# Group-2 projections of tiles 4 to 7 gathered ahead of tile 6, one attention step at a time in the mixer opening, norms of tiles 4 to 7 at one in four steps

## The reference, cut to what matters

```python
h = rms_norm(x, norm_mix_g)
a_b, a_c, a_v, q, k, v, g_a, g_b = split(h @ w_in)        # 512,512,512, 768,768,768, 1024,1024
y_a = (a_b * causal_dwconv(a_c * a_v)) @ w_proj_a
# attention: 12 heads of 64 in 3 groups; group g looks back over (window, dilation) =
# (128, 1), (512, 4), (2048, 16); the three groups of a head slot are mixed by their softmax denominators
y_b = mixed(attention(q, k, v)) @ w_proj_b
x = x + (sigmoid(g_a + b0) * y_a + sigmoid(g_b + b1) * y_b) @ w_out
h = rms_norm(x, norm_ffn_g)
gate, val = split(causal_dwconv(h @ w_up))
out = rms_norm(x + (silu(gate) * val) @ w_down, final_norm_g)
```

## Time and profile before

| | |
|---|---|
| time before, median of 3 runs | 1995.62 us |
| lowest | 1995.58 us |
| the profiled execution | 1993.38 us |
| its span on the slowest core (core 2) | 1991.5 us |
| spans of the eight cores | 1979.9 to 1991.5 us |
| PE busy in the span | 1939.1 us, 97% |
| DVE, ACT, POOL busy | 57%, 42%, 32% |

### The profile page before, as it was taken

The page is one execution under the profiler, slowest core; times in us unless marked ns, Lnnn a source line. Parts: engine busy times, 40 slices in busy tenths (PEclk is TensorE's granted clock), DMA queues, the critical chain, the costliest instruction groups (busy, mean ns, idle before and its releaser), DMA issues.

```text
span 1991.5 us, 38036 instructions; the slowest of 8 cores (1979.9 to 1991.5 us)
## 1 busy us (share of the span) xinstructions
PE 1939.1 (97%) x11662; PEld 1021.4 (51%) x11662; DVE 1140.3 (57%) x1754; ACT 835.4 (42%) x1679; POOL 645.8 (32%) x1431
## 2 busy tenths in 40 slices
PE   5899989999999999999999999999999999999998
PEld 4566656655555444444445555655444444444443
DVE  2456653565445534435236676858684939577582
ACT  2455663452122222121224554636462627355361
POOL 1544430001111021120234354545452626344341
PEclk9899999999999999999999999999999999999999
DMA  9658988385538624525468933131422222221201
GB/s 174 175 152 204 236 203 143 98 185 126 145 100 178 162 59 124 133 48 136 75 186 184 169 104 80 49 102 54 122 60 84 75 85 70 59 96 33 85 1 53
DMA packets 196045, 229.49 MB, mean 115 GB/s; under 512 B 116916, under 2 KB 139322, under 8 KB 195464
## 3 DMA queue, kind: packets, MB, share of 16 engines
q1 hardware_dynamic: 178056, 192.86, 35.7%
q0 software_dynamic: 17792, 34.20, 11.5%
HBM read 161.90 MB, written 72.57 MB: 118 GB/s over the span
## 4 chain that ended last, share of the span: by engine, by line
PE 88%; DMA 4%; issue 2%; POOL 1%; DVE 1%; ACT 1%; SPq 1%; POOLq 0%; DVEq 0%; ACTq 0%
PE psp L682 61%; PE psp L1610 15%; PE psp L1340 6%; PE psp L688 4%; DMA arena<-w_in 1%; DMA arena<-x_loc 1%; PE psp L581 1%; PE psp L553 1%; DMA v_d<-arena 1%; DMA h_d<-arena 1%; DVE arena L1563 1%; POOL rstd L331 1%; ACT arena L556 1%; PE psp L455 1%; DMA arena<-v_d 0%
## 5 line engine op out<-in xcount | busy, mean ns | idle before, releaser
L682 PE MATMUL psp<-arena 128*128 128x512 bf16 (+4 forms) x6848 | 1340.5, 357 | 4.1 <-DVE arena L265 2.3
L682 PEld LDWEIGHTS psp<-arena 128*128 128x128 bf16 x6848 | 661.9, 98 | 653.8 <-issue 11.2
L1563 DVE SCALAR_TENSOR_TENSOR arena<-psp,fcw_s,arena 128x511 f32<-128x511 f32 (+4 forms) x792 | 519.3, 686 | 77.8 <-ACT arena L1556 23.0
L1610 PE MATMUL psp<-arena 128*128 128x512 bf16 x1408 | 305.7, 379 | 0.3 <-POOL arena L1567 0.2
L1556 ACT ACTIVATE arena<-psp,fcb_s,fcw_s 128x512 f32<-128x512 f32 (+1 forms) x396 | 285.7, 730 | 0.8 <-issue 0.4
L1578 POOL TENSOR_TENSOR arena<-arena 128x512 bf16<-128x512 bf16 (+1 forms) x198 | 221.1, 1117 | 66.3 <-ACT uc L1554 18.3
L432 ACT ACTIVATE arena<-arena 128x1024 bf16<-128x1024 f32 (+1 forms) x114 | 120.0, 1053 | 267.1 <-DVE arena L1635 252.5
L1610 PEld LDWEIGHTS psp<-arena 128*128 128x128 bf16 x1408 | 137.6, 98 | 166.5 <-issue 1.2
L1299 DVE TENSOR_TENSOR arena<-psp,arena 128x512 f32<-128x512 f32 (+2 forms) x144 | 90.3, 632 | 223.8 <-PE psp L682 219.2
L1285 ACT ACTIVATE arena<-psp,bg_s 128x512 f32<-128x512 f32 (+2 forms) x144 | 92.0, 640 | 277.2 <-PE psp L682 274.7
L1303 POOL TENSOR_TENSOR arena<-arena 128x512 bf16<-128x512 f32 (+2 forms) x72 | 82.5, 1146 | 278.5 <-DVE arena L1299 223.1
(11 more groups left out here) (88 smaller groups left out, 957.5 us busy)
## 6 DMA issues: line engine op xcount, KB each, us to landing
arena<-x_loc SPq DMA_DIRECT2D x80, 512.0 KB, 5.7
arena<-x_d SPq DMA_DIRECT2D x64, 512.0 KB, 4.1
h_d<-arena SPq DMA_DIRECT2D x65, 256.0 KB, 5.2
x_d<-arena SPq DMA_DIRECT2D x32, 512.0 KB, 6.0
out<-arena SPq DMA_DIRECT2D x32, 512.0 KB, 2.6
u_d<-arena SPq DMA_DIRECT2D x96, 132.0 KB, 5.9
arena<-u_d SPq DMA_DIRECT2D x32, 396.0 KB, 4.6
arena<-w_up POOLq DMA_DIRECT2D x22, 512.0 KB, 17.0
```

Source lines behind the costliest of these rows:

```text
L682: S.add("pe", lambda e, kc=kc: e.matmul(out, lhsT=wap[:, kc, col0:col0 + 128], rhs=rhs(kc), start=(kc == 0), stop=(kc == kcn - 1), skip_gr ...
L1563: S.add("dve", lambda e, b=b, t=t, sh=sh, wv_=wv_, lo=lo: e.scalar_tensor_tensor(out=tmpC[t][:, lo:n], in0=ps[b][:, o + lo - sh:w_ - sh], ...
L1610: S.add("pe", lambda e: e.matmul(ps[b], lhsT=at[:, bi * 128:(bi + 1) * 128], rhs=wt[:, kk, hf * 512:(hf + 1) * 512], start=(k_ == 0), stop ...
```

## The change

- **Group 2 of segment 2.** Tile 4 keeps only its group-2 values; its group-2 keys and queries move behind the products of tile 5. There all of segment 2 follows in one run: keys and queries of 4, values, keys and queries of 5, values of 6, values of 7, keys and queries of 6 and of 7. This needs the transposed `hTA` of tiles 6 and 7 before their own products begin. The list `att2` of segment 1 must be empty there, no longer in tile 4.
- **Group-2 steps.** Segment 1 is worked off at 1.1 steps per tick, then at rates with new horizons (18 in tile 4, 30 in tile 5). Segment 2 is pushed at the start of tile 6 and spread over tiles 6 and 7 (rates of list length by 22 and by 11).
- **Norms.** From the 33rd block on (tile 4 on) a block is begun in one of four ticks.
- **Mixer opening.** Steps are issued singly (`step`), all on bank pair 3 (banks 6 and 7), and the products take banks 0 to 5.

```diff
--- before.py
+++ after.py
@@ -520,7 +520,7 @@
             normed[0] = True
             later(1, load_conv)
         if tickno[0] >= 8:
-            ncred[0] = min(ncred[0] + (0.5 if ns[0] < 9 else 1/2.8), 1.5)
+            ncred[0] = min(ncred[0] + (0.5 if ns[0] < 9 else 1/2.8 if ns[0] < 33 else 0.25), 1.5)
         if ns[0] < len(NBL) and ns[0] - nm[0] < 2 and (force or ncred[0] >= 1):
             ncred[0] -= 1
             stat(ns[0])
@@ -565,6 +565,7 @@
         note("dve", 750)
 
     score_pairs = [2, 3]
+    step = [2]
     ua_ring = deque(range(7))
 
     def ua_next():
@@ -592,7 +593,8 @@
 
     def att_tick():
 
-        n = min(2, len(att) + len(att2))
+
+        n = min(step[0], len(att) + len(att2))
         if n == 0:
             if not pend:
                 return False
@@ -614,8 +616,8 @@
         return True
 
     def att_run():
-        while credit[0] >= 2.0 or credit[0] >= 1.0 and len(att) + len(att2) < 2:
-            credit[0] -= max(1.0, min(2, len(att) + len(att2)))
+        while credit[0] >= step[0] or credit[0] >= 1.0 and len(att) + len(att2) < step[0]:
+            credit[0] -= max(1.0, min(step[0], len(att) + len(att2)))
             if not att_tick():
                 credit[0] = 0.0
 
@@ -857,29 +859,25 @@
         sl, qs = (t + 1) % 3, t % 2
         s, jj = 1 + t // 4, t % 4
 
-        def values2():
+        def values2(t):
+            need(t)
             for half in range(2):
-                v_2(ht, hkeys, s, jj, half, 0)
+                v_2(hTA[slot_of[t]], hk(slot_of[t]), 1 + t // 4, t % 4, half, 0)
                 tick()
-            if jj == 3:
-                later(2, lambda: v2_load(s))
-        def keys2():
+            if t % 4 == 3:
+                later(2, lambda: v2_load(1 + t // 4))
+
+        def keys2(t):
+            ht, hkeys = hTA[slot_of[t]], hk(slot_of[t])
             for c in range(2):
-                k_2(ht, hkeys, s, jj, c)
+                k_2(ht, hkeys, 1 + t // 4, t % 4, c)
                 tick()
-                q_2(ht, hkeys, s, jj, c)
+                q_2(ht, hkeys, 1 + t // 4, t % 4, c)
                 tick()
-        if t == 7:
-            values2()
-            keys2()
-            while att:
-                att_tick()
-            rate[0] = 0.0
-
-            def go2():
-                push_g2(2)
-                rate[0] = 1.7
-            later(3, go2)
+
+        if t == 6:
+            push_g2(2)
+            rate[0] = (len(att) + len(att2)) / 22
         v01_ones(sl, False)
         content["V", sl] = t
         for blk in range(4):
@@ -902,16 +900,26 @@
         if t == 7:
             while att2 or pend:
                 att_tick()
+        if t == 5:
+            while att2:
+                att_tick()
         if t > 0:
             push01(t)
-        if t != 7:
-            values2()
-        if t == 4:
-            while att2:
-                att_tick()
-        if t != 7:
-            keys2()
-        done_tiles.add(t)
+        if t < 5:
+            values2(t)
+        if t < 4:
+            keys2(t)
+        if t == 5:
+            keys2(4)
+            done_tiles.add(4)
+            values2(5)
+            keys2(5)
+            values2(6)
+            values2(7)
+            keys2(6)
+            keys2(7)
+        if t != 4:
+            done_tiles.add(t)
 
     def halo(groups):
 
@@ -985,11 +993,13 @@
         push_g0(t)
         push_g1(t)
         i = SEQ.index(t) + 1
-        horizon = {6: 15, 7: 11}.get(t, 20)
+        horizon = {4: 18, 5: 30, 7: 11}.get(t, 20)
         while i < len(SEQ) and SEQ[i] in units:
             horizon += units[SEQ[i]]
             i += 1
         rate[0] = 1.0 if t == 3 else (len(att) + len(att2)) / horizon + 0.01
+        if t == 6:
+            rate[0] = (len(att) + len(att2)) / 11
 
     wC, wG = [], [None] * 4
     wG_col = (3840, 4864, 3840 + 512, 4864 + 512)
@@ -1109,7 +1119,7 @@
                 sec = halo((2,))
                 later(3, lambda: sec(2))
                 push_g2(1)
-                rate[0] = 1.6
+                rate[0] = 1.1
             later(2, go)
 
     UA.extend(buf("UA%d" % i, R4 + 12288 + (i - 7) * 1056, [128, 4 * VW], F32) for i in range(7, 14))
@@ -1466,6 +1476,9 @@
             tickno[0] += 1
             ub_step(True)
 
+    score_pairs[:] = [3]
+    step[0] = 1
+    pool_main["banks"] = list(range(6))
     for c in range(4):
         conv_c(0, c)
     conv_c(1, 0)
```

## The result

The changed kernel takes 2010.38 us (median of 4 runs, 2010.02 to 2011.07) beside 1996.11 of the kernel before: a ratio of 1.0073, with a 95% interval of 1.0053 to 1.0093. That is 14 us or 0.7% slower, where +4.8 us (1998) was forecast; it lies in the range of 1980 to 2013 and outside the forecast's own of 1990 to 2003. Now and then an execution is slower by several per cent, whatever the kernel: the ratios leave such executions out, the medians of times do not. The profile is that of core 6, whose span is 2008.7 us.

A forecast was written before the change was run, and what follows sets the result against it. PE was taken as full except at 240-280 and 420-440 us, about 15 us to win back. Terms -8.2 - 3.1 + 16.1 = +4.8 on 1993.4 gave 1998 us; own range 1990 to 2003, wider range 1980 to 2013.

The forecast's parts named there:

- Rival B: Tiles 6 and 7: SP's queue stuck, stores of group-2 values free the V2n buffers late; +10 us, 2008; chance 0.15.
- C: Wait for segment 1's values stays (2006), or the mixer opening goes to its bad end (2008); chance 0.10.
- +16.1 for tile 7's values: PE waits 13.3 us there for the last transposing load, caught in the weight-load burst, plus 2.8 us of low clock.
- rival A: No wait at tile 7's values, the last transposing load landing within 12.4 us; 1982 us; chance 0.25.
- The first term (-8.2): At 240 to 280 us, slower norms remove PE's 5.36 us wait for segment 1's values and 2.8 us of low clock.
- the 2304 KB: Transfers no longer ahead of the load of segment 1's values on SP's queue with slower norms; 9.9 us at 238 GB/s.
- The opening (-3.1): Mixer opening, 420 to 440 us: six banks and single steps remove two bank waits, 1.24 and 1.88 us.
- Gathering at nothing: Gathering group 2 in tile 5 only moves products, their number unchanged; counted as 0 us.

The follow-up runs named there:

- the second run of the change: The unaltered change measured once more beside the kernel before on the same chip: 2002.66 us beside 1990.88, ratio 1.0064.

## Why the prediction was right or wrong

**The sign, the place and the mechanism were right, the largest term was too small.** The time came out near the 2008 of rivals B and C, but neither made it: no wait for segment 1's load is left, and the stores cost 2.3 us of PE. The sum had +16.1 for tile 7's values. The slowest core lost 24.3 there, the mean core 23.1 and 21.2. Its parts:

- The landing, 25.7 us after the loads by the row of the kernel before, was 25.6. The mechanism is the one forecast, packet against packet. On this the trace and the Trainium skill ("DMA: Bandwidth & Descriptors", section "SWDGE vs HWDGE vs iDMA") agree: each engine goes round between the queues that the two kinds of issue feed. The figure of 9 to 17 descriptors to a turn that the Trainium skill gives ("DMA: Bandwidth & Descriptors", section "Queues, rings and completion order") I took for a case of rival A. It is one only if the weights' queue takes fewer at its own turn: with as many on both sides the load would be held up just as long, and the equal counts, 690 to 684 and 1079 to 1075, tell nothing of it. The starts of the packets in the change do: they alternate one by one, as far as a packet of the trace is one of the page's descriptors.
- That the two landings agree to a tenth is luck. Over the cores and both runs of the change the last transposing load lands 23.1 to 29.9 us after the weight loads are issued, and in two runs of the kernel before the first of the two that fall into the burst 20.9 to 28.4 us after. Nor was the load alone ahead of its queue, as I took it to be: the pieces of two stores of results went first, until some 327 us.
- PE came to tile 7's values 9.6 us after the loads (328.40 - 318.76), not 12.4. I counted one half of tile 5's values and four products of its keys and queries behind the `mul`; only three of those products were left. DVE ran that `mul` 2.05 us late for POOL's small operations, later against PE than its place in the order says. That makes 2.8 of the missing 8.2 us.
- Rival B came in small on top of the forecast, where I had it as an alternative: the stores of group-2 values stuck behind the transposing load, and copies and PE waited 2.3 us more (4.0 in the second run of the change). B's own sum took 7 us for the landing of those stores, which no row has; in the kernel before they took 8.5 to 8.8, which makes its 10 some 12.
- The clock cost 5.8 us, not 2.8. I took the price of a 5 us wait for one of 16; here two stretches of 20 us passed at 0.81 and 0.68.

**The first term (-8.2) had about the right size and the wrong reason.** 240 to 280 us lost 8.7 in the mean before and 1.1 after, -7.6, of which 1.2 are given back at 231 us. But slower norms alone are worth nothing that the time shows (0.9999), and without them the change still takes away 4.5 to 5.7 of it, by the pace of 1.1. I had that as one more projection ahead of the use, 1.7 us, and gave the weight to the 2304 KB. Both do it, each nearly alone, in two ways: with the slower norms the load of values lands 6.9 us after its issue, and 5.7 in the change, where it takes 8.6 to 9.5 with the old ones; the pace moves the use. Together they are more than the wait. And the slower norms are what put the last transposing load six ticks ahead of its use, beside the whole burst.

**The opening (-3.1) was right:** 7.1 to 3.3 in the change, 4.3 alone, with the waits named. The time of that run alone doesn't tell it from no gain (0.9958 to 1.0001).

**Gathering at nothing** was right: with the norms early the kernel is at 0.9953, and in the change itself tiles 6 and 7 (about 363 to 427 us) lost nothing:

```profile
360.00:380.00 20.00, 20.00 (x179) 13.49 (x178) 7.35 (x12) 7.22 (x10) 0.00 (x0) 1.00 0.44 120
380.00:400.00 20.00, 20.00 (x214) 12.24 (x212) 10.01 (x18) 10.43 (x14) 0.00 (x0) 1.00 0.22 60
400.00:420.00 20.00, 20.00 (x268) 13.43 (x267) 14.27 (x25) 13.56 (x18) 1.49 (x2) 1.00 0.70 144
```

**Sum.** By mean cores: +1.2 - 7.6 - 0.6 + 23.1 - 3.8 = +12.3, near to the 11.8 and 14.3 us measured; the forecast's terms gave +4.8. Of the 7.5 us between, 7.0 are the tile 7 term's.

Rival A's price was about right as well, though its condition (an early landing in the change) did not come: without the collision the kernel is at 0.9953 to 0.9964, 7 to 9 us below the kernel before, where A had 11.

**What beats both kernels** is the change with its old rate of norms: 1981.4 us beside 1989.87, 0.9953 (0.9933 to 0.9974), and again 0.9963 (0.9949 to 0.9976).

## What to carry to other kernels

When a consumer is moved forward in the order, follow its last load through the queues and look for a bulk transfer that the same event sets off: a row of the kernel before may already show the collision where it still costs nothing. Moving the burst only moves the wait to whatever small transfers stand next to it; issuing the small transfer long before its use is what helped, in runs where half of the burst also went later. A first use that is one product later can do the work of megabytes fewer ahead of it, so test the two apart before one is kept for its supposed gain.

## What the runs showed of the hardware that was not expected

- Beside a burst from the other queue a small piece costs one packet of that queue: a 256 KB transposing load that takes 3.0 to 4.9 us without the burst took 21.9 beside packets of 2048 B (690 to 684 packets) and 13.9 beside packets of 512 B (1079 to 1075), and for some 6 of the 13.9 us something else, still open, held it.
- The clock's loss after a wait grew with it: 5.8 us about 18.6 us of idle PE (0.81 and 0.68), where 2.8 went about 7.1 us of the kernel before (5.4 of them one wait).
